# A 269-tile float32 layer stack on one core: the first RMS norm moved behind two projection tiles

## The reference, cut to what matters

```python
def rms_norm(x, g):
    y = x * rsqrt(mean(x * x, axis=-1) + 1e-6)
    return y * g

def first_block(x, norm_g, w_in, ...):
    h = rms_norm(x, norm_g)
    proj = h @ w_in                      # 6656 columns, 52 tiles of 128
    u = proj[..., 0:1024]                # tiles 0 to 7 of the stream
    u = causal_depthwise_conv(u, conv_w, conv_b)          # 4 taps
    r = sigmoid(block_diag(u, w_a) + b_a)                 # one 128x128 block for each tile of u
    i = sigmoid(block_diag(u, w_x) + b_x)
    ...                                  # a scan, attention, gates, a residual
def second_block(...):                   # attention with top-k, short convolution, two SwiGLU layers
```

## Time and profile before

| what | us |
|---|---|
| median of three runs | 1710.96 (1708.39 to 1712.0) |
| the profiled execution | 1710.71 |
| its span, first to last instruction | 1708.9 |
| TensorE busy in the span | 1679.5 (98%) |
| VectorE, ScalarE, GpSimd busy | 1018.7, 699.2, 76.7 |
| mean granted TensorE clock | 0.995 of full speed |

### The profile page before, as it was taken

The page is one execution under the profiler, slowest core; times in us unless marked ns, Lnnn a source line. Parts: engine busy times, 40 slices in busy tenths (PEclk is TensorE's granted clock), DMA queues, the critical chain, the costliest instruction groups (busy, mean ns, idle before and its releaser), DMA issues.

```text
span 1708.9 us, 23305 instructions
## 1 busy us (share of the span) xinstructions
PE 1679.5 (98%) x7891; PEld 1338.1 (78%) x7891; DVE 1018.7 (60%) x2010; ACT 699.2 (41%) x1323; POOL 76.7 (4%) x62
## 2 busy tenths in 40 slices
PE   9999999999999999899999999999999999999999
PEld 7788777778887776577888888887888788888887
DVE  7578776667667788846655653466444633333334
ACT  5365676653343346744333323234223433322322
POOL 0020000000000173100000000000000000000000
PEclk9999999999999999999999999999999999999999
DMA  6232444445541120011655553453333233333333
GB/s 257 62 102 87 172 148 148 148 141 198 190 129 51 54 83 26 1 45 56 221 196 194 181 204 99 135 172 89 96 99 99 76 97 99 99 99 90 95 100 110
DMA packets 56776, 202.84 MB, mean 119 GB/s; under 512 B 6576, under 2 KB 6704, under 8 KB 56560
## 3 DMA queue, kind: packets, MB, share of 16 engines
q1 hardware_dynamic: 56688, 201.68, 35.9%
HBM read 198.38 MB, written 2.10 MB: 117 GB/s over the span
## 4 chain that ended last, share of the span: by engine, by line
PE 89%; DVE 7%; ACT 2%; issue 1%; DMA 0%; DVEq 0%; ACTq 0%; SPq 0%
PE bank L485 26%; PE bank L487 25%; PE bank L486 25%; PE bank L612 2%; PE bank L671 2%; PE bank L650 1%; PE bank L528 1%; PE bank L529 1%; DVE WORK L2008 1%; DVE SM L2007 1%; DVE SB L2091 1%; DVE W_lo L1481 1%; PE bank L531 1%; PE bank L534 1%; PE bank L543 1%
## 5 line engine op out<-in xcount | busy, mean ns | idle before, releaser
L485 PE MATMUL bank<-H_hi,W_hi 128*128 128x512 f32 x1336 | 533.6, 399 | 2.0 <-DVE W_lo L1481 1.0
L486 PE MATMUL bank<-H_lo,W_hi 128*128 128x512 f32 x1336 | 520.5, 390 | 0.0
L487 PE MATMUL bank<-H_hi,W_lo 128*128 128x512 f32 x1336 | 520.5, 390 | 0.0
L1481 DVE TENSOR_TENSOR W_lo<-RAW,W_hi 128x512 fp32r<-128x512 f32 x538 | 353.2, 695 | 175.2 <-ACT W_hi L966 158.9
L966 ACT ACTIVATE W_hi<-RAW 128x512 fp32r<-128x512 f32 x538 | 317.2, 625 | 266.5 <-PE bank L487 236.3
L485 PEld LDWEIGHTS bank<-H_hi,W_hi 128*128 128x128 f32 x1336 | 250.7, 188 | 71.1 <-issue 16.8
L486 PEld LDWEIGHTS bank<-H_lo,W_hi 128*128 128x128 f32 x1336 | 250.9, 188 | 54.7 <-issue 4.8
L487 PEld LDWEIGHTS bank<-H_hi,W_lo 128*128 128x128 f32 x1336 | 250.8, 188 | 53.4
L487 PE MATMUL bank<-A_hi,W_lo 128*128 128x512 f32 x352 | 136.9, 389 | 0.0
L486 PE MATMUL bank<-A_lo,W_hi 128*128 128x512 f32 x352 | 136.9, 389 | 0.0
L485 PE MATMUL bank<-A_hi,W_hi 128*128 128x512 f32 x352 | 136.9, 389 | 0.0
(11 more groups left out here) (272 smaller groups left out, 2061.5 us busy)
## 6 DMA issues: line engine op xcount, KB each, us to landing
RAW<-weights SPq DMA_DIRECT2D x269, 512.0 KB, 3.7
AW<-ada SPq DMA_DIRECT2D x100, 512.0 KB, 3.7
X<-x_t SPq DMA_DIRECT2D x4, 512.0 KB, 5.6
y_t<-X SPq DMA_DIRECT2D x8, 256.0 KB, 2.0
LW<-lru_w SPq DMA_DIRECT2D x1, 1024.0 KB, 12.3
QX<-QR SPq DMA_DIRECT2D x40, 16.0 KB
CROW<-crow SPq DMA_DIRECT2D x1, 512.0 KB, 10.3
ROPE<-rope SPq DMA_DIRECT2D x1, 512.0 KB, 13.1
```

Of the source, the lines that this page charges most:

```text
L485: pe.matmul(dst, wh, ch(hi, k), start=(k == 0), stop=False)
L486: pe.matmul(dst, wh, ch(lo, k), start=False, stop=False)
L487: mm = pe.matmul(dst, wl, ch(hi, k), start=False, stop=(k == chunks - 1))
L1481: dve.tensor_tensor(W_lo[:, w], RAW[:, c:c + HALF], W_hi[:, w], ALU.subtract).then_inc(lo_done, 1)
```

## The change

The norm's sums no longer stand before the first projection. TensorE multiplies tiles 0 and 1 by x*g, not by the normed x, and their results are multiplied by the row factor when VectorE takes them from banks 5 and 6. The pair of tiles that follows the norm chunk by chunk is now 2 and 3. In detail:

- **Loads:** weight tile 0 goes ahead of X, tile 1 ahead of the constants; `crow`, `LW`, the rotation tables and the first `ada` tiles are issued later, between later weight tiles.
- **ScalarE** loads its square root table early, splits tile 0, and for each chunk copies x*g rounded into YA_hi; it squares only the even chunks. It copies the projection tiles 2 to 7 from their banks into Q (`u_out`), and the row factors from bank 2 into SS. The Silu of `crow` moves behind tile 20's weights.
- **GpSimd** squares the odd chunks and adds them up, makes one low half of tile 0, and all low halves of tiles 2 to 8 (`low_half`).
- **VectorE** makes the low parts of x*g (`raw_lo`), the other three low halves of tiles 0 and 1, adds the squares of the even chunks and GpSimd's sum; then it runs the norm as before. The convolution reads Q in SBUF, not the bank.
- **TensorE** runs 20 matmuls on ones, 16 chunks of tiles 0 and 1 by a written order (`raw_chunk`) with the sums over partitions (`first_sums`) after chunk 4 of tile 1, then the spread of the row factor, the pair of tiles 2 and 3, and tiles 4 to 7 with the gates behind them in groups: 0; 1 and 2; 3 and 4; 5. Gates 6 and 7 stay inside tile 8.

```diff
@@ -402,17 +404,13 @@
                              ada[ds(a, 1), :, :].rearrange("a p c -> (a p) c")).then_inc(ada_in[slot], 16)
 
             sp.dma_start(PR[:], prm).then_inc(prm_in, 16)
+            raw(Tile(0), False)
             for k in range(4):
                 sp.dma_start(X[:, 2 * k * S:2 * (k + 1) * S], x[:, 2 * k * S:2 * (k + 1) * S]).then_inc(x_in[k], 16)
-            raw(Tile(0), False)
+            raw(Tile(1), False)
             sp.dma_start(CS[:], cst).then_inc(consts_in, 16)
-            for n in range(1, 4):
-                raw(Tile(n), False)
-            sp.dma_start(CROW[:], crow).then_inc(crow_in, 16)
-            sp.dma_start(LW[:], lru_w).then_inc(lru_in, 16)
-            sp.dma_start(ROPE[:], rope1).then_inc(rope_in, 16)
-            for a in range(4):
-                ada_load(a, a, False)
+            raw(Tile(2), False)
+            raw(Tile(3), False)
 
             def swap_halves(c):
 
@@ -440,6 +438,13 @@
                 if T_Q < t <= T_Q + 10:
                     swap_halves(t - T_Q - 1)
                 raw(Tile(t + 4))
+                if t == 1:
+                    sp.dma_start(LW[:], lru_w).then_inc(lru_in, 16)
+                if t == 4:
+                    sp.dma_start(CROW[:], crow).then_inc(crow_in, 16)
+                    sp.dma_start(ROPE[:], rope1).then_inc(rope_in, 16)
+                if T_Q <= t < T_Q + 4:
+                    ada_load(t - T_Q, t - T_Q, False)
                 if t in ADA_AT:
                     ada_load(ADA_AT[t] % 4, ADA_AT[t] + 4)
                 if t == T_MA:
@@ -589,6 +594,7 @@
                     pe.wait_ge(gate_out, 2 * i)
                 else:
                     pe.wait_ge(lru_in, 16)
+                    pe.wait_ge(u_raw, 1)
                 pe.matmul(ps[3][:], LW[:, j * P:(j + 1) * P], ch(U, j), start=True, stop=True)
                 pe.matmul(ps[4][:], LW[:, (KC + j) * P:(KC + j + 1) * P], ch(U, j),
                           start=True, stop=True).then_inc(gate_mm, 1)
@@ -674,14 +680,47 @@
                 mm.then_inc(pv_mm, 1)
 
 
-            busy(30, None)
-            pe.wait_ge(consts_in, 16)
-            square_sums(0, (SS,), False, (ss_step, 6))
-            norm_stat(0, None, (ss_step, 7))
-            linear_pair(T_U, 0, 5)
-            for t in range(T_U + 2, T_Q):
-                linear(Tile(t), H_hi, H_lo, own=t > 2)
-                gates(t - 2)
+            def first_sums():
+                pe.wait_ge(consts_in, 16)
+                pe.wait_ge(ss_step, 4)
+                for n in range(NB):
+                    mm = pe.matmul(ps[4][:, n:n + 1], SS[:, n * P:(n + 1) * P], cs("sel_all"), start=True, stop=True)
+                mm.then_inc(stat_mm, 1)
+
+            def raw_chunk(tile, dst, k):
+
+                if k % 4 == 0:
+                    pe.wait_ge(lo_done, tile.n * 2 + k // 4 + 1)
+                c = ((2 * tile.slot + k // 4) % 4) * HALF + (k % 4) * P
+                wh, wl = W_hi[:, c:c + P], W_lo[:, c:c + P]
+                pe.wait_ge(raw_hi_done, k + 1)
+                pe.matmul(dst[:], wh, ch(YA_hi, k), start=(k == 0), stop=False)
+                pe.matmul(dst[:], wl, ch(YA_hi, k), start=False, stop=False)
+                pe.wait_ge(raw_lo_done, k + 1)
+                mm = pe.matmul(dst[:], wh, ch(YR_lo, k), start=False, stop=(k == KC - 1))
+                if k % 4 == 3:
+                    mm.then_inc(used, 1)
+
+            pe.sem_inc(bank_free[0], 2)
+            pe.sem_inc(bank_free[1], 1)
+            busy(20, None)
+            for k in range(6):
+                raw_chunk(Tile(0), ps[5], k)
+            raw_chunk(Tile(1), ps[6], 0)
+            raw_chunk(Tile(0), ps[5], 6)
+            raw_chunk(Tile(1), ps[6], 1)
+            raw_chunk(Tile(0), ps[5], 7)
+            for k in range(2, KC):
+                raw_chunk(Tile(1), ps[6], k)
+                if k == 4:
+                    first_sums()
+            pe.wait_ge(rinv_done, 1)
+            stat_rows(16, 2).then_inc(stat_mm, 1)
+            linear_pair(2, 0)
+            for t, todo in ((4, (0,)), (5, (1, 2)), (6, (3, 4)), (7, (5,))):
+                linear(Tile(t), H_hi, H_lo)
+                for i in todo:
+                    gates(i)
             linear(Tile(T_Q), H_hi, H_lo, between=lambda k: gates(6 + k // 4) if k in (1, 5) else None)
             for c in range(1, 10):
                 linear(Tile(T_Q + c), H_hi, H_lo)
@@ -1005,14 +1044,31 @@
 
             act.wait_ge(prm_done, 1)
             act.activation(COL[:, 88:96], COL[:, 80:88], ACT.Exp).then_inc(prm_done, 1)
+            act.wait_ge(ones_done, 1)
+            act.activation(VK[:, 0:1], MG_hi[:, 0:1].bitcast(F32), ACT.Sqrt)
+            split_hi(Tile(0))
             for k in range(KC):
                 if k % 2 == 0:
                     act.wait_ge(x_in[k // 2], 16)
-                square(k, k)
-            split_hi(Tile(0))
-            split_hi(Tile(1))
+                act.activation(ch(YA_hi, k), ch(X, k), ACT.Copy, scale=pr("norm_g", k)).then_inc(raw_hi_done, 1)
+                if k % 2 == 0:
+                    if k >= 4:
+                        act.wait_ge(ss_step, 1)
+                    act.activation(ch(SQ, k // 2 % 2), ch(X, k), ACT.Square).then_inc(sq_done, 1)
+                if k == 5:
+                    split_hi(Tile(1))
+            split_hi(Tile(2))
+            split_hi(Tile(3), (0,))
             root(0, 1)
-            norm_hi(0, None, Tile(2))
+            act.sem_inc(sq_done, 4)
+            for k in range(KC):
+                if k == 2:
+                    split_hi(Tile(3), (1,))
+                if k == 7:
+                    split_hi(Tile(4), (0,))
+                act.wait_ge(t1_done, k + 1)
+                act.copy(ch(H_hi, k), ch(G1, k % 2)).then_inc(h_hi_done, 1)
+            act.copy(SS[:, :], ps[2][:]).then_inc(rows_out, 1)
 
             def gates_out(i):
                 j = U_ORDER[i]
@@ -1020,12 +1076,24 @@
                 act.activation(ch(R, j), ps[3][:], ACT.Sigmoid, bias=pr("b_a", j)).then_inc(gate_out, 1)
                 act.activation(ch(I, j), ps[4][:], ACT.Sigmoid, bias=pr("b_x", j)).then_inc(gate_out, 1)
 
-            split_hi(Tile(2), (1,))
-            act.wait_ge(crow_in, 16)
-            act.activation(CROW[:], CROW[:], ACT.Silu).then_inc(crow_done, 1)
-            for t in range(T_U + 2, T_Q):
-                split_hi(Tile(t + 1))
-                gates_out(t - 2)
+            def u_out(t):
+                tile = Tile(t)
+                ready(tile)
+                act.copy(ch(Q, t), ps[PAIR_BANK if t == 2 else tile.bank][:]).then_inc(u_raw, 1)
+                if t > 2:
+                    act.wait_ge(u_raw, t - 1)
+                    act.sem_inc(bank_free[tile.bank], 1)
+
+            split_hi(Tile(4), (1,))
+            u_out(2)
+            u_out(3)
+            split_hi(Tile(5))
+            for t, todo in ((4, (0,)), (5, (1, 2)), (6, (3, 4)), (7, (5,))):
+                u_out(t)
+                if t < 7:
+                    split_hi(Tile(t + 2))
+                for i in todo:
+                    gates_out(i)
 
             def evac1(c):
                 tile = Tile(T_Q + c)
@@ -1140,6 +1208,8 @@
                 act.sem_inc(bank_free[t % 2], 1)
 
             ga_n = [0]
+            act.wait_ge(crow_in, 16)
+            act.activation(CROW[:], CROW[:], ACT.Silu).then_inc(crow_done, 1)
             for q in range(2):
                 split_hi(Tile(T_GA + q + 1))
                 ga_out(T_GA + q, q)
@@ -1396,12 +1466,35 @@
 
         @block.gpsimd
         def _(pool):
-            pool.memset(YA_hi[:, 0:S].bitcast(F32), 1.0).then_inc(ones_done, 1)
+            pool.memset(MG_hi[:, 0:S].bitcast(F32), 1.0).then_inc(ones_done, 1)
             pool.memset(HALF_NEG[:, 0:1], -0.5).then_inc(pool_chain, 1)
             for x in QX1[:2]:
                 pool.memset(x[:, :], 0.0).then_inc(pool_chain, 1)
             pool.memset(QX1[2][:, :], 0.0).then_inc(x1_zero, 1)
             pool.wait_ge(pool_chain, 3)
+
+            def low_half(tile, half):
+                sl = (2 * tile.slot + half) % 4
+                pool.wait_ge(hi_done, tile.n * 2 + (half + 1))
+                c = tile.slot * TILE + half * HALF
+                w = slice(sl * HALF, (sl + 1) * HALF)
+                pool.tensor_tensor(W_lo[:, w], RAW[:, c:c + HALF], W_hi[:, w], ALU.subtract).then_inc(lo_done, 1)
+
+            for i, k in enumerate((1, 3, 5, 7)):
+                pool.wait_ge(x_in[k // 2], 16)
+                pool.tensor_tensor(ch(R, k), ch(X, k), ch(X, k), ALU.mult).then_inc(odd_sq, 1)
+                if i == 0:
+                    pool.wait_ge(lo_done, 1)
+                    low_half(Tile(0), 1)
+                else:
+                    pool.wait_ge(odd_sq, i + 1)
+                    if i > 1:
+                        pool.wait_ge(odd_sum, i - 1)
+                    pool.tensor_tensor(ch(R, 1), ch(R, 1), ch(R, k), ALU.add).then_inc(odd_sum, 1)
+            pool.wait_ge(lo_done, 4)
```

(67 more changed lines are left out.)

## The result

The changed kernel takes 1718.59 us (median of 5 executions, 1716.71 to 1718.98) against 1710.66 beside it (1708.39 to 1712.0): a ratio of 1.0048, 95% interval 1.0037 to 1.0059. The prediction was 1717.0, slower, range 1708.5 to 1721.5. The profiled execution has a span of 1717.2 us, 8.3 more than before.

What follows compares the result with a forecast made beforehand. TensorE's list of work was taken as the bound: pair start 14.4 later, one pair less -10.9, pair length 0, gate stalls +2.8, together +6.3 us on 1710.7, giving 1717.0 us, range 1708.5 to 1721.5.

Steps and rivals of the forecast that it cites:

- What bounds the kernel: Whole span: TensorE, busy 98%, is the clock; a shift of tile 8's start moves the end by as much.
- The round of GpSimd and VectorE: Opening: the two engines take turns on SBUF operands, eight rounds of 1.72 us; sum of squares ready at 25.1.
- The start of the pair: Tiles 2 and 3 after the norm: first product at 33.7 us, 14.4 later than the earlier pair's 19.34.
- the clock's term: Opening, chunks of tile 1: a fall of TensorE's granted clock costs 0 to 3.0 us; 1.5 taken.
- The pair's length: Tiles 2 and 3: +2.1 (GpSimd holding two low halves) against -1.4 (full clock instead of half); 0 taken for both.
- The gates: Gates 2 and 4, directly behind 1 and 3, wait for ScalarE's sigmoids: two stalls of about 1.4 us, +2.8.
- What is hidden: Copies to Q, later low halves on GpSimd, the convolution on SBUF, moved loads and Silu: covered, adding 0.
- A: Opening: GpSimd does not hold VectorE; pair starts at 24.3, time 1706.2 us, faster; chance 0.12.
- B: Opening: half of GpSimd's eight operations do not hold VectorE and the clock holds; +0.7, 1711.4 us; chance 0.22.
- C: Opening into the pair: clock falls and stays low, +1.5 and +1.4 more, 1719.9 us; chance 0.18 together with D.
- D: Pair: GpSimd's low halves of tiles 2 and 3 come late; counted on C's side, chance 0.18 together.

Runs made afterwards that it cites:

- e4: Changed kernel with GpSimd's four squares and three sums of the opening replaced by memsets, which read nothing from SBUF; 1710.33 us, ratio 0.9999.
- a9: The changed kernel with no edit, measured and profiled once more; 1717.48 us, ratio 1.0044.
- e5: Changed kernel with ScalarE's squares of chunks 4 and 6 given buffers of their own, so it need not wait for the first add; 1716.21 us, ratio 1.0037.
- e10: The same kernel as e5, run again side by side with a9; 1716.66 us, ratio 1.0040.
- e6: Changed kernel with ScalarE squaring all chunks, TensorE summing each, GpSimd idle in the opening, row factor spread earlier, gates as in e1; 1707.24 us, ratio 0.9991.
- e1: Changed kernel with gates 2 and 4 moved from behind gates 1 and 3 into the middle of tiles 6 and 7; 1714.37 us, ratio 1.0023.
- e2: Changed kernel with GpSimd's opening work removed: ScalarE squares all chunks, VectorE makes the sums and tile 0's second low half; 1711.14 us, ratio 1.0006.
- e3: Changed kernel with 34 matmuls on ones filling TensorE's waits in tile 0's chunks 0 to 5; 1716.44 us, ratio 1.0035.

## Why the prediction was right

Sign and mechanism held, and the size (7.9 measured between the medians, 6.3 predicted). In the profiles the 6.3 became 8.3: -0.4 at the start of the pair, +0.7 in its length, +0.3 at the gates, +0.4 of small pieces and +1.0 behind tile 8. That the start of the pair is met within 0.4 is partly luck, since several errors cancel in it. By its steps:

- **What bounds the kernel.** Right. Of the 8.3 us of span, 7.26 are the shift of tile 8. The other 1.0 had no term. The stretch behind tile 8 lasts 1633.3 to 1635.5 in the profiles of these kernels, 1633.9 before and 1634.9 after; whether this 1.0 is the change's was not settled.
- **The round of GpSimd and VectorE: mis-sized.** I took 1.72 from the earlier trace rows; in the steady part it is 1.57. Three of the GpSimd operations there are squares, which read the same chunk twice, and last 1.48; the sums, with two chunks, 1.60. I counted eight rounds from 7.3. VectorE's first `raw_lo` began only at 8.28, for GpSimd's first square had held an operation on the parameters; its eight operations up to 20.03 took 11.75 and not 13.76, the six behind them 3.81 and not 4.1. +1.0 - 2.0 - 0.3 is the 1.3 us by which the sum came early (23.84, predicted 25.1). That VectorE is held was right; e4 shows it for the squares and sums by taking the reads away.
- **The start of the pair: 33.37, predicted 33.7.** The sum was 1.3 early; the clock cost 2.5 where I had set 1.5 within 0 to 3.0. Two terms between them were misread, and with the wait ahead of the narrow sums they cancel: the eight records at 12.49 in the earlier trace rows are the four sums themselves, which here take 0.81 (28.07 to 28.88) and not 0.6, and the 3.05 from the spread to the pair had passed at half clock; at full clock they are 2.31 (31.06 to 33.37). a9 shows 32.04 for the same code, e5 and e10 show 30.77 and 31.83: the clock's term is not a number but a spread, and both bounds were needed.
- **The pair's length: mis-sized.** I took 0 for +2.1 and -1.4, though these add to +0.7, and gave no reason; it was +0.67, but by other sizes. Two low halves of the pair lasted 1.7 and 1.8 us beside GpSimd's, and TensorE waited 1.3 for them. In e6, where VectorE makes the low halves of tiles 2 and 3 itself, the pair takes 11.50 and not 10.9: by that the full clock gave 0.8 of the 1.4, and the holding cost 1.5 of the 2.1.
- **The gates: 3.1, predicted 2.8.** Right in place and cause; e1 takes back 3.17. Each wait is 1.5 and not 1.4.
- **What is hidden.** Right where a row shows it: TensorE has no new wait between the pair and tile 8 but the two for a sigmoid. I had not seen ScalarE's wait of 3.37 us; e5's sum stands only 0.2 earlier without it, and e10's time is not told apart from a9's.
- **The rivals.** A (no holding) did not happen, but e4 is its experiment: A's pair was worked out to start at 24.3, and e4's starts at 24.51. A's time was not met: 1706.2 against 1710.33, since the pair takes 13.01 and not 10.9 (+2.1), the stretch behind tile 8 is 1634.9 (+1.0), and the gates and small pieces take most of the rest. B (half holding) and C (clock at half into the pair) did not happen; the clock was back before the pair in every profile. Nor did D: TensorE had no wait for a weight's low half in the pair.

## What to carry to other kernels

Where VectorE's operations have two SBUF operands, one of them moved to GpSimd, where it reads SBUF too, relieves VectorE of about 0.65 us and then holds another of its operations by 0.8 to 1.0: here the opening got longer by 4.6 us for it (26.27 to 30.87, both at full clock). Count it as a cost wherever VectorE paces the path, and look for the room elsewhere: with that work on ScalarE, VectorE and TensorE, the row factor spread earlier, and two gates moved apart, the same change went from 0.5% slower to 0.3% faster. And when a step slows the feed of TensorE, add the clock as a spread: with late operands it fell to the lower level here in five profiles of five, and with earlier ones (e2, e4) or with the waits filled (e3) it did not.

## What was not expected of the hardware

- A GpSimd operation that only writes SBUF (memset, 0.53 us) does not hold VectorE: 0.68 to 0.74 beside it, against 1.5 to 1.76 beside squares and sums. The Trainium skill (SBUF — State Buffer, section "SBUF: two separate sides") says of VectorE's operations with two SBUF inputs that they meet GpSimd's only where these read SBUF; e4 agrees. The Trainium skill says in the same section that the loser is blocked for the whole instruction. The 128x8 operation of VectorE at 6.43 agrees: it lasts 1.05 us in place of 0.17 and ends with GpSimd's square. But a round is shorter than the two durations one behind the other: 1.25 + 0.69 = 1.94 with a GpSimd operation on two chunks, 1.04 + 0.69 = 1.73 with a square; the trace has 1.57, and that decides.
- A square on GpSimd with the same chunk as both operands took 1.04 us in the one case in which VectorE did not delay it (6.42), against 1.25 for a product of two chunks.
- The granted clock came back at 18.7, 22.9, 23.5, 25.9 and 26.5 us in executions in which TensorE had been given the same work (e5, e10, a9, changed kernel, e1).
